# Convolution and gate steps moved into the projection, and delta rule products reordered, in a two-layer hybrid trunk

## The chip, the cores and the metric

One NeuronCore of a Trainium2 chip runs the whole program; nothing is shared with other cores. The metric is device time in microseconds for one execution. The core has five engines that work side by side and meet through semaphores: TensorE (PE, the 128x128 array, with its weight loads shown apart as PEld), VectorE (DVE), ScalarE (ACT), GpSimd (POOL) and SyncE (SP), which here only issues DMAs.

## The reference, cut to what matters

Two layers (`DEPTH = 2`) run over 512 latent and 256 context tokens of width 1024, in fp32. Each layer modulates and projects the tokens to 3088 columns, runs three mixers on slices of them (softmax attention, a gated delta rule, HGRN2), projects back, and then runs a mixture of 16 experts. The second layer gives no output for the context tokens.

```python
q, k, v = split(silu(conv5(cols['dn_qkv'])))          # depthwise, 5 taps, 768 channels
f = lb + (1 - lb) * sigmoid(cols['hg_f'])             # HGRN2 forget gates
# gated delta rule, per head and chunk of 64 tokens (4 heads, 12 chunks, 2 directions)
m    = where(strict, (k*beta) @ k.T * decay, 0)
u, w = solve(I + m, [v*beta, k*beta*exp(cum)])        # unit triangular, 64x64
v_new = u - w @ state
out   = (q*exp(cum)) @ state + (q @ k.T * decay) @ v_new
state = state*exp(c_last) + (k*exp(c_last - cum)).T @ v_new
```

Attention has 8 query heads of 64 over 2 key/value heads. A latent query tile of 128 tokens sees all 768 keys, a context query tile sees the 256 context keys.

## The kernel before, in words

The 768 tokens are six tiles of 128 (tiles 0 and 1 are context, 2 to 5 latent); a tile holds two chunks of 64 tokens, one on partitions 0 to 63 and one on 64 to 127. The program is written by hand, engine by engine: every engine has its own list of functions that runs the stages of a layer in order (modulation, norm, projection, attention, delta rule, HGRN2, output projection, norm, experts), and the order inside a list is the order in which that engine works. Nothing is planned by a tool. What an engine waits for is written as semaphore waits.

**Projection.** `pe_proj` runs 48 units of 8 matmuls (L687) in 8 column groups, through six PSUM banks; `act_proj` (L615) evacuates each unit. Group boundaries fall at units 12 (queries, keys and values done), 24 (the six convolution input tiles `convin` done), 30, 38, 42 (HGRN2 gates `hgc` done) and 48. `dve_attention` prepares queries and keys from unit 12 on, and then waits for unit 48 (`projev` 48) before it does anything else, because its output tile `convout` lay over the second buffer of the weight ring, which the projection still uses.

**Attention.** A unit is one head of one query tile: 48 units in layer 0 (16 of context tiles, then 32 of latent tiles) and 32 in layer 1 (latent only). PE does the scores (L918), six or two transposes of the probabilities (L931) and the product with the values (L941); DVE takes the row maximum (L816) and part of the copy (L825), ACT the exponential (L882) and the rest of the copy (L895). Between them DVE runs one of the 30 convolution steps (L846, L849) in each of the first 30 units and one of the 4 gate steps (L860) in each of the first 4.

**Delta rule.** `act_deltanet` begins with six silu activations over `convout` (L1148) and goes on with the gates (L1149 to L1154). PE waits for the last silu and for the last attention output, then transposes `convout` into token tiles (L1216). DVE squares and sums them (L985, L986). Then for each of the two directions `d`:

- cumulative gates and decays (L1240, L1241), and the gram products (L1251), each followed by DVE work per tile;
- six levels of a doubling scheme for the triangular inverse. In a level, DVE masks the six tiles (L1039), PE multiplies by `small_products` (L1261), ACT copies the result (L1190), PE multiplies twice more (also L1261; once in the last level, not at all in level 0), and DVE subtracts (L1058). The next level's masks come after all six subtractions, in DVE's own order;
- the solution `Y` with 128 columns (L1261 again), copied by ACT (L1194);
- the transition matrices (L1312, L1314, L1317), taken up by DVE (L1068) and ACT (L1202, L1204), then 11 dependent steps over the chunks (L1327, L1079);
- the outputs: per tile the products with the state (L1351, L1353), DVE's fresh values (L1092 to L1098), and the product with the local attention matrix (`apply_values`, L1261 again), added by DVE (L1107, L1109).

All of these products are 64x64 blocks: contraction over 64 partitions (the lower or upper half of the rows of the array) and an output on 64 partitions (the lower or upper half of its columns). The trace shows two matmul instructions, each with its own weight load, for one fp32 product. So a call of `small_products` with 8 products is 16 instructions, and a level of 18 calls is 288. `HB[0]` and `HB[1]` are the two halves. In `small_products` both the row half and the column half are `HB[par]`: before the change four products in a row go to one half, then four to the other.

**What follows.** HGRN2 (L1532 and on), the output projection (L1602) and the experts (L1775, L1803) are not touched.

## Time and profile before

| | us |
|---|---|
| median of 3 runs | 4424.52 |
| range of these runs | 4422.88 to 4425.82 |
| the profiled execution, its own time | 4431.7 |
| span from first to last instruction in it | 4429.9 |

| engine | busy us | share | instructions |
|---|---|---|---|
| PE | 3673.1 | 83% | 24115 |
| PEld | 2632.4 | 59% | 24115 |
| DVE | 2318.7 | 52% | 3029 |
| ACT | 1813.0 | 41% | 2325 |
| POOL | 340.9 | 8% | 100 |

Busy time is the union of an engine's instructions. PE's ends are modelled, so an instruction that has started 0.1 us after another overlaps it, and a busy PE is not PE at its peak; how many instructions are done in a stretch says more. PEclk is the clock that TensorE is granted, as a share of 2.4 GHz; it has two levels, 1.0 and 0.5, and a value between them is a mean over a stretch. An idle time in brackets is that of the engine just before the row, with what ended it.

### The profile page before, as it was taken

The numbers are of one execution on the slowest core, as the hardware profiler recorded it, in microseconds if no ns is written. First come the engines' busy times: TensorE is split into PE (matmuls) and PEld (weight loads), VectorE is DVE, ScalarE is ACT, GpSimd is POOL, SyncE is SP. The second block draws the span as 40 slices with busy tenths as digits, with TensorE's granted clock in tenths as the row PEclk, the third lists the DMA queues.
The fourth block names the chain that finished last, engine by engine and source line by source line (L and its number), as shares of the span: only waits on it lengthen the run. The fifth ranks groups of instructions, "written<-read, shape, count | busy, mean of one in ns | idle before, by whom it ended". The sixth has DMA issues, their size and how long they took to land.

```text
span 4429.9 us, 59181 instructions
## 1 busy us (share of the span) xinstructions
PE 3673.1 (83%) x24115; PEld 2632.4 (59%) x24115; DVE 2318.7 (52%) x3029; ACT 1813.0 (41%) x2325; POOL 340.9 (8%) x100
## 2 busy tenths in 40 slices
PE   6999997776849889988888999887767577887777
PEld 1565777775526666666634657687664366666666
DVE  0112325558446777777731203345583577777767
ACT  1112222113126677777621112311232467767766
POOL 0000000000011111111100000000000112121111
PEclk9998557685879999999999995576757788888888
DMA  7210000000147888888863100000002688878775
GB/s 256 75 39 19 0 1 2 2 2 2 39 167 289 307 327 318 307 306 309 303 220 120 53 19 1 1 2 2 2 2 85 239 292 316 317 294 301 297 299 210
DMA packets 180696, 680.12 MB, mean 154 GB/s; under 512 B 15435, under 2 KB 25759, under 8 KB 180383
## 3 DMA queue, kind: packets, MB, share of 16 engines
q1 hardware_dynamic: 166088, 637.81, 37.8%
q0 software_dynamic: 6144, 20.98, 2.0%
q10 hardware_dynamic: 8283, 18.67, 1.1%
q8 instruction: 144, 2.36, 0.2%
q14 instruction: 37, 0.30, 0.0%
HBM read 656.44 MB, written 20.97 MB: 153 GB/s over the span
## 4 chain that ended last, share of the span: by engine, by line
PE 61%; DVE 16%; DMA 9%; issue 7%; ACT 6%; ACTq 1%; SPq 0%; DVEq 0%; POOL 0%; PEldq 0%
PE ps L687 11%; PE ps L1803 11%; PE ps L1775 8%; DMA gu<-in_moe_w_up 7%; PE ps L1261 6%; PE ps L918 4%; PE ps L941 4%; PE ps L1602 3%; DVE down_lo L2010 3%; ACT hi L1865 3%; DVE gu_lo L2010 2%; PE ps L641 2%; DMA arena<-in_w_mod 2%; PE ps L931 2%; PE ps L1810 1%
## 5 line engine op out<-in xcount | busy, mean ns | idle before, releaser
L2010 DVE TENSOR_TENSOR gu_lo<-gu,hi 128x2816 fp32r<-128x2816 f32 x256 | 782.7, 3087 | 354.3 <-ACT hi L1865 354.3
L1865 ACT ACTIVATE hi<-gu 128x2816 fp32r<-128x2816 f32 x256 | 640.4, 2549 | 136.0 <-DMA gu<-in_moe_w_up 127.3
L1775 PE MATMUL ps<-hi,xsplit 128*96 128x512 f32 (+3 forms) x2304 | 576.4, 397 | 99.7 <-ACT hi L1865 88.2
L1775 PEld LDWEIGHTS ps<-hi,xsplit 128*96 128x96 f32 (+1 forms) x2304 | 411.8, 183 | 230.6 <-ACT hi L1865 108.2
L2010 DVE TENSOR_TENSOR down_lo<-down,hi 128x1024 fp32r<-128x1024 f32 (+1 forms) x256 | 417.5, 1654 | 172.5 <-ACT hi L1865 172.5
L687 PE MATMUL ps<-arena 128*128 128x512 f32 (+2 forms) x1536 | 501.7, 488 | 7.1 <-PE ps L687 4.3
L1775 PE MATMUL ps<-gu_lo,xsplit 128*96 128x512 f32 (+3 forms) x1536 | 416.4, 410 | 85.9 <-DVE gu_lo L2010 85.2
L687 PEld LDWEIGHTS ps<-arena 128*128 128x128 f32 x1536 | 290.5, 190 | 217.1 <-issue 191.7
L1775 PEld LDWEIGHTS ps<-gu_lo,xsplit 128*96 128x96 f32 (+1 forms) x1536 | 282.0, 192 | 194.6 <-DVE gu_lo L2010 133.2
L1865 ACT ACTIVATE hi<-down 128x1024 fp32r<-128x1024 f32 (+1 forms) x256 | 343.6, 1373 | 123.4 <-PE ps L1803 123.2
L1261 PE MATMUL ps<-arena 64*64 64x64 f32 (+1 forms) x6080 | 266.1, 234 | 27.0 <-DVE arena L1039 21.5
L1261 PEld LDWEIGHTS ps<-arena 64*64 64x64 f32 x6080 | 258.5, 140 | 31.8 <-DVE arena L1039 24.3
L2095 POOL DMA_INDIRECT arena<-xn_rows,row_of x32 | 78.4, 2451 | 2514.2 <-DVE row_of L2001 2505.3
L816 DVE TENSOR_REDUCE nmax<-ps 128x1 f32<-128x768 f32 (+1 forms) x80 | 68.0, 850 | 349.5 <-PE ps L918 349.5
L615 ACT ACTIVATE arena<-ps 128x256 f32<-128x256 f32 (+3 forms) x132 | 49.7, 403 | 445.6 <-PE ps L687 445.5
L941 PEld LDWEIGHTS ps<-arena 128*128 128x128 f32 x832 | 183.3, 329 | 54.1 <-issue 48.8
L641 PE MATMUL ps<-arena,condT 128*2 128x512 f32 x384 | 173.6, 606 | 44.6 <-DMA arena<-in_w_mod 21.7
L918 PE MATMUL ps<-arena 64*128 64x256 f32 (+1 forms) x288 | 202.3, 850 | 2.8 <-ACT arena L874 2.8
L1532 PE MATMUL ps<-arena 64*64 64x64 f32 x2688 | 130.7, 315 | 85.5 <-DVE arena L1413 85.5
L941 PE MATMUL ps<-arena 128*128 128x64 f32 x832 | 198.4, 426 | 3.3 <-ACT arena L895 3.3
L1532 PEld LDWEIGHTS ps<-arena 64*64 64x64 f32 x2688 | 122.5, 219 | 93.5 <-issue 55.8
L882 ACT ACTIVATE arena<-ps,nmax 128x768 f32<-128x768 f32 (+1 forms) x80 | 65.3, 816 | 227.7 <-DVE nmax L816 227.6
(292 smaller groups left out, 4986.6 us busy)
## 6 DMA issues: line engine op xcount, KB each, us to landing
gu<-in_moe_w_gate SPq DMA_DIRECT2D x256, 704.0 KB, 6.1
gu<-in_moe_w_up SPq DMA_DIRECT2D x256, 704.0 KB, 8.0
down<-in_moe_w_down SPq DMA_DIRECT2D x64, 2048.0 KB, 7.9
arena<-in_w_mod SPq DMA_DIRECT2D x24, 2048.0 KB, 7.7
down<-in_moe_w_down SPq DMA_DIRECT2D x32, 1536.0 KB, 9.8
arena<-in_w_in SPq DMA_DIRECT2D x6, 2048.0 KB, 7.6
arena<-in_w_out SPq DMA_DIRECT2D x4, 2048.0 KB, 9.8
arena<-in_w_in SPq DMA_DIRECT2D x4, 1536.0 KB, 7.3
```

The costliest lines, as they stand in the source:

```text
L641: ins = nc.tensor.matmul(ps[0:2, g % 2, :], lhsT=cT[:, f, :], rhs=w[:, f, :], start=(f == 0), stop=(f == KT - 1))
L687: ins = nc.tensor.matmul(out, lhsT=lhs, rhs=rhs, start=(f == 0), stop=(f == KT - 1))
L918: ins = nc.tensor.matmul(ps[:, b + n0 // 512, 0:n], lhsT=qkT[part, j, qt * P:(qt + 1) * P], rhs=qkT[part, 4, n0:n0 + n], start=True, stop= ...
L931: ins = nc.tensor.transpose(out, prob[u % 2][:, kt * P:(kt + 1) * P], ident)
L941: ins = nc.tensor.matmul(ps[:, 6 + u % 2, 0:HD], lhsT=probT[u % 2][:, kt * P:(kt + 1) * P], rhs=vtok[:, kt, kv * HD:(kv + 1) * HD], start= ...
L1261: ins = nc.tensor.matmul(ps[HB[par], bank, c0 + width * h:c0 + width * (h + 1)], lhsT=lhs[HB[par], i, h, :], rhs=rhs(par, h), start=True, ...
L1532: ins = nc.tensor.matmul(ps[HB[c % 2], 2 * (n % 3) + hb, c // 2 * HD:c // 2 * HD + HD], lhsT=a, rhs=b, start=True, stop=True)
L1602: ins = nc.tensor.matmul(ps[:, u % 6, :], lhsT=yT[:, f, i * P:(i + 1) * P], rhs=w[:, f, :], start=(f == 0), stop=(f == KT - 1))
L1775: ins = nc.tensor.matmul(ps[0:lhs.shape[1], 3 * m + b, 0:n], lhsT=lhs, rhs=w[:, c0 + 512 * b:c0 + 512 * b + n], start=(row == 0 and stage ...
L1803: ins = nc.tensor.matmul(ps[0:lhs.shape[1], 3 + half, :], lhsT=lhs, rhs=w[:, c0:c0 + 512], start=(ft == 0 and stage == 0 and n == 0), stop ...
L1865: nc.scalar.activation(hi_part(u), whole(u), ACT.Copy).then_inc(hi_a.sem, 1)
L2010: nc.vector.tensor_tensor(lo_part(u), whole(u), hi_part(u).bitcast(F32), ALU.subtract) \
```

## The change

The convolution steps and the gate steps of DVE leave the attention loop. All 30 convolution steps now follow the preparation of queries and keys, after a wait for unit 24, and the 4 gate steps follow a wait for unit 42. The six silus move from the head of `act_deltanet` into `act_proj`, ahead of unit 42. For that `convout` gets a place of its own instead of lying over the weight ring, and `rope2` and `sq_dn` move with it. Layer 0 takes the latent query tiles (2 to 5) first and the context tiles (0, 1) last; layer 1 keeps its order. The loops of four groups of products are turned, so that consecutive products go to different halves of the array. The products themselves, their operands and their number stay as they are.

```diff
-        rope2 = view(extra, 640)
+        rope2 = view(36752, 640)
...
-        convout = view(10752, 6, 772)
+        convout = view(38984, 6, 772)
         dt = view(0, NT, 768)
-        sq_dn = view(extra, NT, 512)
+        sq_dn = view(7680, NT, 512)
...
+                if u == 42:                                                   # act_proj
+                    for j in range(6):
+                        act.wait_ge(conv.sem, conv.n(layer, 24 + j + 1))
+                        nc.scalar.activation(convout[:, j, :], convout[:, j, :], ACT.Silu).then_inc(convact.sem, 1)
...
-            qt, h = divmod(u + 48 - attn_units(layer), NQ)                    # attn_unit
+            qt, h = divmod(u + NQ * NT_CTX, NQ)
+            qt %= NT
...
-            dve.wait_ge(projev.sem, projev.n(layer, 48))                      # dve_attention
+            dve.wait_ge(projev.sem, projev.n(layer, 24))
...
+            for n in range(30):
+                conv_step(n)
+            dve.wait_ge(projev.sem, projev.n(layer, 42))
+            for u in range(4):
+                f = hgc[:, 2 + u, :]
+                nc.vector.tensor_scalar(f, f, omlT[:, layer, u:u + 1], lbT[:, layer, u:u + 1], ALU.mult, ALU.add) \
+                    .then_inc(f_v.sem, 1)
...
             for u in range(attn_units(layer)):
-                if u < 30:
-                    conv_step(u)
-                if u < 4:
-                    f = hgc[:, 2 + u, :]
-                    nc.vector.tensor_scalar(f, f, ...).then_inc(f_v.sem, 1)
...
-            for j in range(6):                                                # act_deltanet
-                act.wait_ge(conv.sem, conv.n(layer, 24 + j + 1))
-                nc.scalar.activation(convout[:, j, :], convout[:, j, :], ACT.Silu).then_inc(convact.sem, 1)
...
                     for hb in range(2):                                       # gram products, L1251
-                        for par in range(2):
-                            c = 2 * i + par
-                            for pair in range(2):
+                        for pair in range(2):
+                            for par in range(2):
+                                c = 2 * i + par
...
                 def small_products(bank, c0, lhs, rhs, i, width=64):
-                    for par in range(2):
-                        for h in range(DNH):
+                    for h in range(DNH):
+                        for par in range(2):
                             ins = nc.tensor.matmul(ps[HB[par], bank, c0 + width * h:c0 + width * (h + 1)],
                                                    lhsT=lhs[HB[par], i, h, :], rhs=rhs(par, h), start=True, stop=True)
...
                         for pair in range(2):                                 # transitions, L1312 to L1317
                             for hb in range(2):
-                                h = 2 * pair + hb
-                                out = ps[HB[hb], 2 * (i % 2) + par, :]
+                                h, out = 2 * pair + hb, ps[HB[hb], 2 * (i % 2) + par, :]
                                 nc.tensor.matmul(out[:, 64 * pair:64 * pair + 64], lhsT=vke[HB[par], i, h, HD:2 * HD],
                                                  rhs=TR[HB[par], i, 1, h, :], start=True, stop=True)
+                            for hb in range(2):
+                                h, out = 2 * pair + hb, ps[HB[hb], 2 * (i % 2) + par, :]
...
+                            for hb in range(2):
+                                h, out = 2 * pair + hb, ps[HB[hb], 2 * (i % 2) + par, :]
...
                     for hb in range(2):                                       # outputs, L1351 and L1353
-                        for par in range(2):
-                            c = 2 * i + par
-                            for pair in range(2):
-                                out = ps[HB[par], 2 * (i % 2) + hb, :]
+                        for pair in range(2):
+                            for par in range(2):
+                                out, c = ps[HB[par], 2 * (i % 2) + hb, :], 2 * i + par
                                 nc.tensor.matmul(out[:, 64 * pair:64 * pair + 64], lhsT=ykT[HB[hb], i, pair, par, :],
                                                  rhs=S[HB[hb], c, pair, :], start=True, stop=True)
+                            for par in range(2):
+                                out, c = ps[HB[par], 2 * (i % 2) + hb, :], 2 * i + par
```

## Rows read from the trace of the kernel before

**Rows 1.** The page: busy time by engine; granted clock in 40 slices.
```profile
PE 3673.1 (83%) x24115; PEld 2632.4 (59%) x24115; DVE 2318.7 (52%) x3029; ACT 1813.0 (41%) x2325; POOL 340.9 (8%) x100
PEclk9998557685879999999999995576757788888888
```

**Rows 2.** The page: lines of the chain that ended last.
```profile
PE ps L687 11%; PE ps L1803 11%; PE ps L1775 8%; DMA gu<-in_moe_w_up 7%; PE ps L1261 6%; PE ps L918 4%; PE ps L941 4%; PE ps L1602 3%; DVE down_lo L2010 3%; ACT hi L1865 3%; DVE gu_lo L2010 2%; PE ps L641 2%; DMA arena<-in_w_mod 2%; PE ps L931 2%; PE ps L1810 1%
```

**Rows 3.** Windows (us, PE, PEld, DVE, ACT, POOL busy, clock, DMA): attention, delta rules.
```profile
396.00:665.00 269.00, 264.29 (x862) 184.68 (x862) 99.02 (x226) 72.40 (x160) 0.00 (x0) 0.52 0.00 1
665.00:991.00 326.00, 256.08 (x4772) 240.38 (x4772) 173.01 (x493) 65.27 (x175) 0.00 (x0) 0.77 0.01 2
2862.00:3190.00 328.00, 258.57 (x4580) 242.91 (x4580) 165.69 (x466) 65.11 (x175) 0.00 (x0) 0.72 0.01 2
```

**Rows 4.** Groups by line (busy us, mean ns | idle before): a convolution step.
```profile
L849 DVE SCALAR_TENSOR_TENSOR arena<-arena,rowsT 128x772 f32<-128x772 f32 x48 | 48.7, 1014 | 0.0
```

**Rows 5.** Windows in attention: units with a convolution step, units without.
```profile
450.00:460.00 10.00, 10.00 (x29) 6.29 (x29) 4.64 (x10) 2.07 (x4) 0.00 (x0) 0.50 0.01 2
560.00:570.00 10.00, 10.00 (x29) 6.29 (x28) 2.70 (x8) 2.19 (x4) 0.00 (x0) 0.50 0.01 2
```

**Rows 6.** Timeline (start, us, row, idle before), ACT: the first copy of unit 42.
```profile
361.19 0.38 ACT L615 ACTIVATE arena<-ps 128x256 f32<-128x256 f32 x1 [6.81 <-PE ps L687]
```

**Rows 7.** Timeline, layer 0: from the last attention output into the delta rule.
```profile
663.18 4.53 ACT L1148 ACTIVATE arena<-arena 128x772 f32<-128x772 f32 x6
664.85 0.28 DVE L832 TENSOR_SCALAR arena<-ps,rinv 128x64 f32<-128x64 f32 x1 [2.70 <-PE ps L941]
667.85 3.55 PE L1216 MATMUL ps<-const,arena 128*128 128x128 f32 x18 [3.11 <-ACT arena L1148]
670.80 0.24 ACT L1154 ACTIVATE gb<-gb 128x48 f32<-128x48 f32 x1
672.09 0.69 DVE L985 TENSOR_TENSOR arena<-arena 128x512 f32<-128x512 f32 x1
```

**Rows 8.** Windows of direction 0, layer 0: levels and solution, transitions, outputs.
```profile
719.35:791.19 71.84, 65.14 (x1536) 63.86 (x1536) 35.07 (x77) 15.11 (x36) 0.00 (x0) 0.96 0.01 3
791.19:811.27 20.08, 14.41 (x289) 13.76 (x289) 13.60 (x49) 4.71 (x24) 0.00 (x0) 0.65 0.01 2
823.29:839.73 16.44, 14.52 (x288) 14.27 (x289) 10.50 (x38) 0.00 (x0) 0.00 (x0) 0.76 0.01 2
```

**Rows 9.** Timeline, PE: level 0, a middle level, the last, the solution; layer 1.
```profile
719.35 6.70 PE L1261 MATMUL ps<-const,arena 64*64 64x64 f32 x96 [4.31 <-DVE arena L1039]
739.15 11.02 PE L1261 MATMUL ps<-arena 64*64 64x64 f32 x288 [1.11 <-DVE arena L1039]
775.56 7.86 PE L1261 MATMUL ps<-arena 64*64 64x64 f32 x192 [1.11 <-DVE arena L1039]
784.02 6.48 PE L1261 MATMUL ps<-arena 64*64 64x128 f32 x96 [0.60 <-DVE arena L1058]
2948.85 12.42 PE L1261 MATMUL ps<-arena 64*64 64x64 f32 x288 [1.11 <-DVE arena L1039]
```

**Rows 10.** Narrow windows of PE, 0.33 us after first start: L1261, then L1327.
```profile
719.67:719.78 0.10, 0.10 (x4) 0.50 0.00 0
811.60:811.70 0.10, 0.10 (x8) 0.50 0.00 0
```

**Rows 11.** Timeline, PE, bursts in other orders: L1327, L1532, L1552.
```profile
811.27 0.69 PE L1327 MATMUL ps<-arena 64*64 64x64 f32 x8 [3.31 <-ACT arena L1204]
1036.07 8.02 PE L1532 MATMUL ps<-arena 64*64 64x64 f32 x192 [0.34 <-DVE arena L1413]
1048.78 1.19 PE L1552 MATMUL ps<-arena 64*64 64x64 f32 x32 [0.21 <-ACT arena L1510]
```

**Rows 12.** Groups by line: DVE's subtraction in a level.
```profile
L1058 DVE TENSOR_TENSOR arena<-arena,ps 128x512 f32<-128x512 f32 x96 | 66.1, 688 | 102.8 <-PE ps L1261 102.8
```

**Rows 13.** Timeline, DVE: fresh values of the third tile wait for PE.
```profile
830.88 0.29 DVE L1092 TENSOR_TENSOR arena<-arena,ps 128x128 f32<-128x128 f32 x1 [1.36 <-PE ps L1353]
```

More of the change, by code:

```diff
@@ L810, in dve_attention, with conv_step @@
             nc.vector.memset(ss[:, 60:61], 0.0).then_inc(qk_ready.sem, 1)
+            nc.vector.memset(convin[:, :, 0:2], 0.0)
+            nc.vector.memset(convin[:, :, 258:262], 0.0)
+            link(nc.vector.memset(convin[:, :, 774:776], 0.0))
+            dve.wait_ge(projev.sem, projev.n(layer, 24))
+            def conv_step(n):
+                k, j = divmod(n, 6)
+                w = rowsT[:, layer * 30 + n:layer * 30 + n + 1]
+                if k == 0:
+                    ins = nc.vector.tensor_scalar(convout[:, j, :], convin[:, j, 0:772], w, None, ALU.mult)
+                else:
+                    dve.wait_ge(conv.sem, conv.n(layer, n - 5))
+                    ins = nc.vector.scalar_tensor_tensor(convout[:, j, :], convin[:, j, k:k + 772], w,
+                                                         convout[:, j, :], ALU.mult, ALU.add)
+                ins.then_inc(conv.sem, 1)
+            for n in range(30):
[5 more added lines that the diff above has]
+                    .then_inc(f_v.sem, 1)
             def row_max(u):
@@ L833, in finish @@
                                         None, ALU.mult).then_inc(attn_y.sem, 1)
-            nc.vector.memset(convin[:, :, 0:2], 0.0)
-            nc.vector.memset(convin[:, :, 258:262], 0.0)
-            link(nc.vector.memset(convin[:, :, 774:776], 0.0))
-            dve.wait_ge(projev.sem, projev.n(layer, 48))
-            def conv_step(n):
-                k, j = divmod(n, 6)
-                w = rowsT[:, layer * 30 + n:layer * 30 + n + 1]
-                if k == 0:
-                    ins = nc.vector.tensor_scalar(convout[:, j, :], convin[:, j, 0:772], w, None, ALU.mult)
-                else:
-                    dve.wait_ge(conv.sem, conv.n(layer, n - 5))
-                    ins = nc.vector.scalar_tensor_tensor(convout[:, j, :], convin[:, j, k:k + 772], w,
-                                                         convout[:, j, :], ALU.mult, ALU.add)
-                ins.then_inc(conv.sem, 1)
             row_max(0)
             for u in range(attn_units(layer)):
-                if u < 30:
-                    conv_step(u)
-                if u < 4:
-                    f = hgc[:, 2 + u, :]
-                    nc.vector.tensor_scalar(f, f, omlT[:, layer, u:u + 1], lbT[:, layer, u:u + 1], ALU.mult, ALU.add) \
-                        .then_inc(f_v.sem, 1)
                 if u + 1 < attn_units(layer):
```

## The prediction

> **What bounds the kernel now.** I read the page first. PE is busy for 83% of the span, and no other engine passes 52%; of the granted clock the reader is to see the 5s in slices 5, 6, 10, 25, 26 and 30: there TensorE has 1.2 GHz and not 2.4 [rows 1]. The chain of waits is mostly PE's; the lines that the change touches hold L1261 at 6% and L918, L941, L931 at 10% together [rows 2]. So I asked for windows by stage. Attention: PE busy 264.3 of 269.0 us at a mean clock of 0.52. Delta rule: 256.1 of 326.0 us at 0.77 in layer 0, 258.6 of 328.0 at 0.72 in layer 1 [rows 3]. No DMA runs in either. Whatever PE or the chain saves there moves all that follows by the same amount, since the experts' loads start only after the output projection. Then the timelines, for which wait ends last at each seam.
>
> **Part 1: convolution and gate steps leave attention.** A step costs DVE 1.014 us or less [rows 4], 30 of them at most 30 us per layer. In attention they are covered: a stretch with steps has PE busy 10.00 of 10 us and 29 matmuls, one without has the same 10.00 and 29, while DVE falls from 4.64 to 2.70 [rows 5]. Their removal there is worth nothing in the steady state. I allow 0.3 us in each layer for the first units, in which DVE's row maximum queues behind them; that is inside the rounding below. In the projection DVE sits idle after the preparation of the queries, PE needs only ACT's evacuations, and 24 units of PE work lie between unit 24 and attention, one of which alone holds ACT idle for 6.81 us [rows 6]. 30 us of steps and four gate steps end well before that. Cost 0; if that cover were gone, up to 30 us a layer. No DMA is moved, and no queue of SP or POOL is passed.
>
> **Part 2: the silus.** Six take 4.53 us, and 1.28 us more for a table load [rows 7]. Ahead of unit 42 ACT is idle for 6.81 us, waiting for PE [rows 6]; 5.8 us fit, and the table load for silu that unit 42 pays now serves both. Were they late, PE has six banks and stops only when an evacuation is five units behind. Cost 0. At the delta rule's head they are on the path: the last attention output ends at 664.85 + 0.28 = 665.13, and the transposes of L1216 start at 667.85 [rows 7], 2.7 us later. ACT then loads a table for Exp (1.28), which it would still hold from attention, and one for Ln. Next late after the change is the chain over the gates: three short DVE operations after 665.13 (some 0.25 us each), an exponential like L1154 (0.24), one load (1.28) and L1154 itself. By this estimate L1154 ends at about 667.7 and not 671.04, and L985 starts at 668.7 for 672.09. Gain 3.4 us a layer, **6.8 us**. From there DVE bounds the stretch, and nothing else is given back.
>
> **Part 3: latent tiles first, layer 0 only.** The units and their products are the same, and PE is full between first and last. What can change is PE's idle time at the two ends, 269.0 - 264.3 = 4.7 us in all [rows 3], so the effect lies between -4.7 and +4.7. A long unit first exposes a longer maximum and exponential, a short one last leaves less to drain. I take **-1.5 us**.
>
> - *Middle levels*, 4 per direction, 16 in all: 288 x 0.029 + 0.3 (the last one's own run) = 8.7 us for 11.02. The 1.11 us ahead of each (DVE's last subtraction 0.69, then the first mask 0.42) stays. DVE's subtractions, 6 x 0.69 [rows 12], and ACT's copies fit in the shorter level. 16 x 2.35 = **37.6**.
> - *Last level*: 192 x 0.029 + 0.3 = 5.9 for 7.86; 4 x 1.9 = **7.6**.
> - *Level 0*: 96 in 6.70, mostly at half clock, 70 ns; alternating 96 x 0.054 + 0.4 = 5.6 us, with DVE's two operations a tile nearly as late. 4 x 1.1 = **4.4**.
> - *Solution*, 128 columns: 96 in 6.48, 67.5 ns; 96 x 0.056 + 0.3 = 5.7, and ACT, busy for 15.1 of 71.8 us here [rows 8], keeps up. 4 x 0.9 = **3.6**.
> - *Transitions*: PE 14.4 and DVE 13.6 of 20.1 us [rows 8]: the two take turns over two pairs of banks. A shorter PE turn (about 0.4 us) counts on every second tile: **4 x 1 = 4**.
> - *Outputs*: 16.4 us, PE 14.5, DVE 10.5 [rows 8]; the third tile's fresh values wait 1.36 us for PE [rows 13]. PE's turn of 48 instructions at up to 70 ns is 2.4 to 3.4 us; at L1532's 42 ns it is 2.0, and DVE's 10.5/6 = 1.75. I take 2.2 us less in each direction, minus 0.7 for a clock that may not rise here as it does now (mean 0.76): 4 x 1.5 = **6**.
> - *Gram products*: DVE is late on both sides of each tile. 0, between -1 and +1.
>
> Sum of part 4: 63.2 us. In transitions and outputs only the column halves alternate, the rows stay. L1552 does just this and runs 32 instructions in 1.19 us [rows 11], so I count them as above. A rule of the Trainium skill speaks against it: "TensorE: Matmul & The Clock Gate", Part 3, has it that a weight load overlaps running matmuls only when its group of rows differs. By the rule these two items would give nothing and the sum would be 10 us smaller. The rule disagrees with L1552 as this trace has it.
>
> **The clock.** The same middle level took 12.42 us in layer 1, against 11.02, where the clock fell to half for a while, after the 1.11 us pause between levels [rows 9]. The change keeps these pauses and brings them closer together (every 9.8 us, not 12.1), so I expect a few more such falls: 3 at 1.4 us, **+4 us**.
>
> **The sum.** -6.8 - 1.5 - 63.2 + 4 = -67.5 us. The profiled execution took 4431.7 us (span 4429.9), so it would take 4364. It is 7.2 us above the median of the runs; the same difference on the median 4424.5 gives **4357 us**. Bounds of the main term: at 27 ns instead of 29 some 10 us more, at 34 ns some 25 us less.
>
> **Rivals.**
>
> - *Instructions can't be fed that fast.* A level would be bound by PE's issue and not by the halves. For it: nothing in the trace sustains 29 ns over 288 pairs; against it: L1532 keeps the array fuller over 192. At 36 ns part 4 falls to some 15 us, with 6.8 and 1.5: 4401 us. Chance 0.10.
> - *The order is already undone by overlap, or only the row halves matter.* Without the two items of fixed rows: 4367, inside the first forecast's range, chance 0.10. With no gain from order at all, 8.3 us remain: 4416, which is -0.19%. Chance 0.03.
> - *Slower: the clock leaves the levels.* The clock is low in attention though PE is busy there for 98%. In the levels it is at 0.96 over 71.84 us [rows 8]. If the denser, shorter levels with the same pauses no longer held it, a middle level would take 288 x 0.054 + 0.3 + 1.11 = 17 us for 12.1, the last +2.7, the solution +4: 26 us a direction, 104 in all, less 20 for the rest: 4509 us. It decides from the point where some 45% of the levels' time runs at half clock. Against it: levels with a 1.11 us pause keep the full clock now in layer 0. Chance 0.04.
>
> **How the numbers follow.** The forecast has 0.73: 4357, own range 4342 to 4378. With the rivals, 4340 to 4400 leaves out about 2 in 10. A difference of 0.2% (9 us) is about what a measurement can tell from none. Faster: all of the forecast, the first rival and the fixed rows, 0.92. Same: 0.03. Slower: 0.05.
>
> **What would show it.** A middle level of 8.4 to 9.0 us with 288 matmuls of L1261 after a pause of still 1.11; L985 about 3.6 us after the last attention output instead of 7.0; DVE busy in the projection and at 2.7 of 10 us in attention; the first attention unit long in both layers; full clock through the levels. It is wrong if a level stays above 10 us, if PE waits for a projection evacuation near unit 42, or if the levels' mean clock falls below 0.8.

## The result, and the profile after

The changed kernel took 4225.42 us (median of four runs: 4223.52, 4225.41, 4225.44, 4380.44), the kernel before on the same chip 4423.7. The ratio is 0.9552, 95% interval 0.9533 to 0.957: 198 us less, where 67.5 were forecast. The direction was right and the time fell outside the range. Each kernel shows two or three separate values, some 90 to 130 us apart, because in each run each of the two attentions has TensorE either at 2.4 GHz or, from its first microseconds on, at 1.2 GHz; the ratio compares the changed kernel's runs with the higher clock in layer 0 with runs of the kernel before that had it in neither layer. The profiled executions show this directly; for a run without a profile, which attention kept the clock is concluded from its time. The experiments are about that.

The page of the profiled execution (4225.41 us, span 4223.6): the engines' busy times, and TensorE's clock in 40 slices.

```profile
PE 3462.4 (82%) x24115; PEld 2456.5 (58%) x24115; DVE 2321.5 (55%) x3029; ACT 1806.0 (43%) x2321; POOL 350.4 (8%) x100
PEclk9999986858799999999899975587557787888888
```

PE has as many instructions as before and is busy 211 us less [rows 1]. Of the two 5s that stood in slices 5 and 6 none is left; those of layer 1's attention (slices 25 and 26) stay. The chain of waits gives less to the small products, now L1266, and to attention, now L949, L926 and L939, than it did [rows 2]; here it is by engine and by line:

```profile
PE 58%; DVE 18%; DMA 9%; issue 7%; ACT 6%; ACTq 1%; SPq 0%; DVEq 0%; POOL 0%; PEldq 0%
PE ps L692 12%; PE ps L1812 11%; PE ps L1784 8%; DMA gu<-in_moe_w_up 7%; PE ps L1266 5%; PE ps L949 3%; PE ps L1611 3%; PE ps L926 3%; DVE down_lo L2019 3%; DVE gu_lo L2019 3%; ACT hi L1874 3%; PE ps L646 3%; DMA arena<-in_w_mod 2%; PE ps L939 2%; PE ps L1819 1%
```

Its lines of attention come to 8% (they were 10%) and L1266 to 5% (6%). Windows by stage show more (us; busy time of PE, PEld, DVE, ACT, POOL; the mean clock; DMA): attention and delta rule of layer 0, then of layer 1.

```profile
399.06:545.66 146.60, 142.91 (x862) 102.99 (x862) 71.70 (x193) 68.08 (x157) 0.00 (x0) 1.00 0.00 1
545.66:850.50 304.84, 217.56 (x4772) 199.16 (x4773) 183.53 (x507) 65.38 (x173) 0.00 (x0) 0.74 0.01 2
2475.61:2701.00 225.39, 221.78 (x735) 158.22 (x735) 55.52 (x129) 56.20 (x109) 0.00 (x0) 0.52 0.00 1
2701.00:2997.60 296.60, 212.45 (x4582) 195.13 (x4583) 176.45 (x481) 65.64 (x173) 0.00 (x0) 0.74 0.01 2
```

Layer 0's attention falls from 271.5 us (396.3 to 667.8) to 146.6, with the clock at 1.00 for all of it and not 0.52 [rows 3]. That is 125 us. The silus account for 2.7 of them and the order of units for about 1; the other 121 come with the clock, and no term of the forecast holds them. Layer 1's attention has the same stream and gained 3 us (228.2 before), the silus again. The delta rule lost 31 us in layer 0 and 42 in layer 1; the forecast had some 33 a layer for the whole of it, of which 2.7 of the silus' 3.4 fall in the attention window. So the part that was worked out came about as said, and one stage did something else.

The delta rule's parts. A timeline of PE through levels and solution of layer 0's first direction (start, us, instruction, count, idle time before):

```profile
596.62 1.97 PE L1266 MATMUL ps<-const,arena 64*64 64x64 f32 x32 [4.31 <-DVE arena L1047]
599.05 3.44 PE L1266 MATMUL ps<-const,arena 64*64 64x64 f32 x64 [0.46 <-DVE arena L1055]
603.42 8.85 PE L1266 MATMUL ps<-arena 64*64 64x64 f32 x288 [0.93 <-DVE arena L1047]
613.39 8.85 PE L1266 MATMUL ps<-arena 64*64 64x64 f32 x288 [1.12 <-DVE arena L1047]
...
643.30 6.28 PE L1266 MATMUL ps<-arena 64*64 64x64 f32 x192 [1.12 <-DVE arena L1047]
650.20 5.46 PE L1266 MATMUL ps<-arena 64*64 64x128 f32 x96 [0.62 <-DVE arena L1066]
```

A middle level takes 8.85 us for 11.02, 30.7 ns an instruction, and the pause ahead of it is still 1.12 us [rows 9]. The windows of the same direction: levels with solution, transitions, outputs.

```profile
596.62:656.34 59.72, 52.42 (x1536) 50.40 (x1536) 34.99 (x77) 15.09 (x36) 0.00 (x0) 0.95 0.02 4
656.34:675.05 18.71, 11.26 (x288) 10.50 (x289) 13.59 (x49) 4.71 (x24) 0.00 (x0) 0.69 0.01 2
687.07:700.75 13.68, 10.82 (x288) 10.11 (x289) 10.28 (x38) 0.00 (x0) 0.00 (x0) 0.74 0.01 2
```

They stood at 71.84, 20.08 and 16.44 [rows 8]. The seam from attention to delta rule, last output (L863) to first square (L993):

```profile
545.32 0.28 DVE L863 TENSOR_SCALAR arena<-ps,rinv 128x64 f32<-128x64 f32 x1 [0.38 <-PE ps L949]
545.66 2.19 PE L1221 MATMUL ps<-const,arena 128*128 128x128 f32 x18 [0.45 <-DVE arena L863]
546.61 1.28 ACT L1159 ACT_TABLE_LOAD   x1
549.19 0.69 DVE L993 TENSOR_TENSOR arena<-arena 128x512 f32<-128x512 f32 x1
```

From the end of L863 to L993 it is 3.6 us; it was 7.0 [rows 7]. One table load is left of the two that stood there. In the projection the steps and silus run while PE works, in groups by line from 145 to 399 us (busy, mean ns, idle before):

```profile
L830 DVE SCALAR_TENSOR_TENSOR arena<-arena,rowsT 128x772 f32<-128x772 f32 x24 | 22.5, 1017 | 0.0
L601 ACT ACTIVATE arena<-arena 128x772 f32<-128x772 f32 x6 | 4.5, 833 | 0.0
```

The projection lasts 253.8 us with them and without: free, as forecast.

Now the head of attention in the changed kernel, twice in one execution: layer 0 (three windows) and layer 1 (three windows), each the pause before the first scores, the first scores, and what follows.

```profile
402.56:403.97 1.41, 0.00 (x1) 0.00 (x1) 0.00 (x0) 1.39 (x5) 0.00 (x0) 1.00 0.00 0
403.97:407.60 3.63, 2.84 (x9) 1.42 (x9) 1.71 (x2) 2.24 (x3) 0.00 (x0) 1.00 0.00 0
407.60:411.27 3.67, 3.67 (x22) 2.69 (x23) 1.59 (x3) 1.76 (x4) 0.00 (x0) 1.00 0.02 4
2479.08:2480.48 1.40, 0.00 (x0) 0.00 (x0) 0.00 (x0) 1.38 (x5) 0.00 (x0) 1.00 0.00 0
2480.48:2482.79 2.31, 2.31 (x7) 1.28 (x8) 0.71 (x1) 1.25 (x1) 0.00 (x0) 1.00 0.00 0
2482.79:2486.00 3.21, 2.83 (x10) 1.78 (x9) 1.51 (x3) 2.23 (x5) 0.00 (x0) 0.50 0.00 0
```

The streams are the same: PE idle for 1.4 us while ACT copies queries and keys, then the same eight score instructions. In layer 0 the clock stays; in layer 1 it falls to 0.50, 2.31 us after the first scores, and stays there to the end of the stage, 218 us in which PE is busy for 99% of the time. Before the change it fell in layer 0 too, 3.29 us after its first scores.

### The profile page after: what moved, and what is told of

It is laid out like the page before. It is cut to its first block, busy times and chain, and to the rows that moved or that the text cites. A ratio compares the mean times of both kernels' runs of the same rounds, so it can differ in the third digit from the quotient of the medians.

```text
span 4223.6 us, 59177 instructions
## 1 busy us (share of the span) xinstructions
PE 3462.4 (82%) x24115; PEld 2456.5 (58%) x24115; DVE 2321.5 (55%) x3029; ACT 1806.0 (43%) x2321; POOL 350.4 (8%) x100
## 4 chain that ended last, share of the span: by engine, by line
PE 58%; DVE 18%; DMA 9%; issue 7%; ACT 6%; ACTq 1%; SPq 0%; DVEq 0%; POOL 0%; PEldq 0%
PE ps L692 12%; PE ps L1812 11%; PE ps L1784 8%; DMA gu<-in_moe_w_up 7%; PE ps L1266 5%; PE ps L949 3%; PE ps L1611 3%; PE ps L926 3%; DVE down_lo L2019 3%; DVE gu_lo L2019 3%; ACT hi L1874 3%; PE ps L646 3%; DMA arena<-in_w_mod 2%; PE ps L939 2%; PE ps L1819 1%
## 5 line engine op out<-in xcount | busy, mean ns | idle before, releaser
L692 PEld LDWEIGHTS ps<-arena 128*128 128x128 f32 x1536 | 290.5, 190 | 217.1 <-issue 191.8
L1266 PE MATMUL ps<-arena 64*64 64x64 f32 (+1 forms) x6080 | 207.7, 225 | 31.6 <-DVE arena L1047 21.6
L1266 PEld LDWEIGHTS ps<-arena 64*64 64x64 f32 x6080 | 197.6, 137 | 40.0 <-DVE arena L1047 24.4
L1541 PEld LDWEIGHTS ps<-arena 64*64 64x64 f32 x2688 | 122.5, 219 | 93.5 <-issue 55.8
L949 PEld LDWEIGHTS ps<-arena 128*128 128x128 f32 x832 | 137.8, 255 | 38.5 <-issue 29.4
L926 PE MATMUL ps<-arena 64*128 64x256 f32 (+1 forms) x288 | 151.6, 657 | 2.8 <-ACT arena L882 2.8
L949 PE MATMUL ps<-arena 128*128 128x64 f32 x832 | 150.4, 347 | 2.4 <-ACT arena L903 2.3
L2126 POOL DMA_INDIRECT out<-arena,row_of x16 | 112.2, 7011 | 441.5 <-DVE arena L2033 441.5
```

Source lines behind the costliest of these rows:

```text
L692: ins = nc.tensor.matmul(out, lhsT=lhs, rhs=rhs, start=(f == 0), stop=(f == KT - 1))
L926: ins = nc.tensor.matmul(ps[:, b + n0 // 512, 0:n], lhsT=qkT[part, j, qt * P:(qt + 1) * P], rhs=qkT[part, 4, n0:n0 + n], start=True, stop= ...
L949: ins = nc.tensor.matmul(ps[:, 6 + u % 2, 0:HD], lhsT=probT[u % 2][:, kt * P:(kt + 1) * P], rhs=vtok[:, kt, kv * HD:(kv + 1) * HD], start= ...
L1266: ins = nc.tensor.matmul(ps[HB[par], bank, c0 + width * h:c0 + width * (h + 1)], lhsT=lhs[HB[par], i, h, :], rhs=rhs(par, h), start=True, ...
L1541: ins = nc.tensor.matmul(ps[HB[c % 2], 2 * (n % 3) + hb, c // 2 * HD:c // 2 * HD + HD], lhsT=a, rhs=b, start=True, stop=True)
L2126: nc.gpsimd.indirect_dma_start(out=table, out_offset=bass.IndirectOffsetOnAxis(ap=row_of[0:rows_e, e:e + 1].bitcast(U32), axis=0), in_=ye[ ...
```

## The experiments

Four theories. **U**: the order of units; long units first leave PE fewer pauses. **V**: the empty DVE, whose steps held up the first row maxima. **C**: chance, how the start of attention falls in time. And, from the second set on, **P**: PE's pauses at the head decide, and afterwards attention holds whichever clock it finds. Times differ by a few us between sets, so each kernel is set against the kernel before in its own set. "Both at half" means both attentions at half clock.

### First set: one part of the change at a time

`e1`: before, with the new order of the products.

```diff
-                    for par in range(2):          # small_products; gram, transitions and outputs likewise
-                        for h in range(DNH):
+                    for h in range(DNH):
+                        for par in range(2):
```

> The kernel before with the new order of the products alone (gram, small products, transitions, outputs); convolution steps, silus and unit order as before. All theories of attention say that nothing happens there: layer 0 attention at about 271 us and half clock. The delta rule should lose what it lost in the whole change less the silus: 31.3 + 41.7 us in the stages of layers 0 and 1, of which about 3.4 a layer are the silus, so 66 us: 4424 - 66 = 4358 us. If the change's delta rule gain came instead from freeing it of the silus and of a clock that was already higher when it began, this run stays above 4390.

`e2`: before, with latent tiles first.

```diff
-            qt, h = divmod(u + 48 - attn_units(layer), NQ)
+            qt, h = divmod(u + NQ * NT_CTX, NQ)
+            qt %= NT
```

> The kernel before with latent query tiles first in layer 0, nothing else. Theory U (order of units: long units leave PE fewer pauses in the first microseconds of attention, and the clock, once kept there, stays full for the whole stage): layer 0 attention about 147 us for 271.5, so 4424 - 125 = 4299 us in most runs. Theory V (it is the empty DVE: with convolution and gate steps between the row maxima PE pauses longer at the start): 4423 us, attention stays at half clock. Theory C (chance: how the start of attention falls against the moments at which the clock changes): some runs near 4423 and some near 4299.

`e3`: before, with the steps and silus moved into the projection.

```diff
-            dve.wait_ge(projev.sem, projev.n(layer, 48))
+            dve.wait_ge(projev.sem, projev.n(layer, 24))
...
+            for n in range(30):
+                conv_step(n)
...
```

> The kernel before with convolution steps, gate steps and silus done during the projection; context tiles first as before, old order of the products. Theory U: attention stays at half clock, only the silus' 6.8 us are gained: 4417 us. Theory V: 4424 - 6.8 - 125 = 4292 us. Theory C: a mix of both values.

`e4`: the changed kernel with context tiles first again.

```diff
-            qt, h = divmod(u + NQ * NT_CTX, NQ)
-            qt %= NT
+            qt, h = divmod(u + 48 - attn_units(layer), NQ)
```

> The changed kernel with context tiles first again in layer 0. Theory U: the attention gain goes, 4225 + 125 = 4350 us in all runs. Theory V: 4225 us stays. Theory C: a mix of 4225 and 4350.

Measured, all runs:

| kernel | both at half | one attention kept |
|---|---|---|
| before | 4426.67 to 4443.99 (9 runs) | 4340.12, 4345.4 |
| e1 | 4351.06, 4354.64, 4360.56 | 4253.99 |
| e2 | 4427.16 to 4437.57 (4) | 4305.27, 4309.13 |
| e3 | 4409.87 to 4438.45 (5) | 4338.1 |
| e4 | 4349.42 to 4356.51 (5) | 4247.38 |

V alone falls: e3 with an empty DVE kept layer 0 in none of its six runs. U in its plain form falls too: e2 kept it in two of six. Even the kernel before has runs 90 us below the rest. The profiled run of e3 tells which attention that is:

```profile
397.25:665.90 268.65, 264.67 (x863) 184.79 (x863) 72.70 (x193) 69.51 (x157) 0.00 (x0) 0.51 0.00 1
2645.58:2769.30 123.72, 119.75 (x734) 87.91 (x734) 55.57 (x128) 56.16 (x109) 0.00 (x0) 1.00 0.00 1
```

Layer 1 took 123.7 us. At half clock and with the silus moved, as in e3, this stage takes 225.4 to 225.7 (the changed kernel, e4), so the clock is worth 102 us there. Against their own kernels the kept runs of before and e3 gain less, 88 to 97 us; part of the difference lies in the levels of the delta rule, which took 294.0 us in before's profile and 301.1 in e3's, and the rest isn't resolved. e2's profiled run is the other kind, with layer 0 at 0.99:

```profile
400.87:552.50 151.63, 142.97 (x862) 103.00 (x863) 97.70 (x229) 73.28 (x163) 0.00 (x0) 0.99 0.00 1
```

So something that differs from run to run has a part in it (C), and the order of units shifts the odds. e1's three runs at half have a median of 4354.6, against 4433.5 for the nine of before: the order of the products alone is worth 79 us and not 66.

### Second set: how often, and the pauses

`f1`: the changed kernel again.

> The changed kernel itself once more, for how often each value comes. Theory C+U (whether the clock falls at the start of an attention is a matter of where that start falls in time, and long units first only make keeping it likelier; one layer each): a mix of 4350 us (both attentions at half clock), 4225 (layer 0 kept, -125), about 4247 (layer 1 kept, -104) and perhaps 4120 (both). Theory U alone (long units first always keep layer 0): 4225 in all but stray runs. Like for like, with both attentions at half clock, the change should be worth 4432 - 4352 = 80 us by the kernel with context tiles first.

`f2`: the changed kernel with filler products in both pauses; `f3` with the first alone. They go to a part of PSUM that nobody reads.

```diff
+            def fill(*widths):
+                for n in widths:
+                    nc.tensor.matmul(ps[:, 7, 0:n], lhsT=ident, rhs=qn[:, 0, 0:n], start=True, stop=True)
+            fill(512, 256)                                    # after the transposes of queries and keys
             pe.wait_ge(qktev.sem, qktev.n(layer, 5))
...
+                if u == 0:
+                    fill(256, 128)                            # f2 only
                 turn(u)
```

> The changed kernel with filler products (their output is never read) in TensorE's two pauses at the head of each attention: 512 and 256 columns in the pause of 1.41 us before the first scores, 256 and 128 in that before the first transposes of probabilities. Theory P (those pauses let the clock fall, and a clock once kept stays for the stage): both attentions at full clock in every run, 4350 - 125 - 104 = 4121 us, with no spread over 20 us. Theory N (the fall depends on the chip's moment alone, or on the half-filled score products and not on the pauses): a mix as in the changed kernel, 4225 to 4355.

> The same with filler products only in the first pause. Theory P with the first pause as the one that matters (five of the six falls seen so far came 1.5 to 2.6 us after the first scores, when only this pause lay behind): 4121 us as with both. If the second pause matters too: now and then 4225 or 4250. Theory N: a mix from 4225 to 4355.

`f4`: the first pause made longer.

```diff
+                if p == 4:
+                    for _ in range(2):
+                        link_act(nc.scalar.activation(qkT[:, p, 0:512], ps[:, b, :], ACT.Copy))
                 nc.scalar.activation(qkT[:, p, 0:512], ps[:, b, :], ACT.Copy)
```

> The changed kernel with the first pause made longer by two more copies of 512 columns on ScalarE ahead of the first scores (about 1 us more in each layer). Theory P: the clock falls in both attentions in every run, 4352 + 2 = 4354 us. Theory C+U without a role of the pause: a mix as in the changed kernel.

| kernel | all runs |
|---|---|
| before | 4429.98 to 4448.58 (9), median 4434.99; 4342.62, 4342.77 |
| f1 | 4343.24, 4349.78, 4355.45, 4356.64; 4230.83, 4232.88 |
| f2 | 4124.54 to 4135.88 (6), median 4130.27 |
| f3 | 4115.72 to 4133.22 (6), median 4123.99 |
| f4 | 4350.4 to 4360.54 (4), median 4354.0 |

P holds on both sides. With 1.3 us of filler the clock stayed in both layers in all 12 runs; with 1.25 us more of idle time it fell in both layers in all four. Filling the second pause adds nothing. (Filler both closes a pause and adds products; no run here separates the two.) f3's timeline of PE at the head of layer 1 (L918 is the filler, 0.12 us before the scores), and its two attentions:

```profile
2484.63 3.46 PE L913 MATMUL ps<-const,arena 128*128 128x128 f32 x30 [0.84 <-ACT arena L620]
2487.93 1.46 PE L918 MATMUL ps<-arena,const 128*128 128x512 f32 x4
2489.51 2.84 PE L931 MATMUL ps<-arena 64*128 64x512 f32 x8
...
```

```profile
396.33:542.90 146.57, 144.20 (x867) 103.70 (x867) 71.71 (x193) 68.09 (x157) 0.00 (x0) 1.00 0.00 1
2484.63:2608.40 123.77, 121.04 (x739) 88.57 (x739) 55.57 (x129) 56.15 (x109) 0.00 (x0) 1.00 0.00 1
```

f1 answers how often: the changed kernel kept layer 0 in 2 of 6 runs here and in 3 of 4 in the first measurement. Over all sets layer 0 was kept in 7 of 16 runs with latent tiles first (the changed kernel, f1 and e2) and in none of 49 with context tiles first (before, e1, e3, e4), all without filler. An empty DVE may help: 5 of 10 without steps in attention, 2 of 6 with them, too few to tell. With equal clocks (both at half) the changed kernel takes 4352.6 us for 4435.0, **82 us less**, where the runs of each spread over 13 and 19 us. That is what the change is worth in itself.

### Third set: the change's part in it, the rule on rows, the dips in the levels

The kernel before took 4425.76 to 4436.78 us here (4 runs, median 4429.3) with both attentions at half clock, and 4327.31, 4332.13 and 4335.99 with one kept.

`g1`: the kernel before with f3's filler.

> The kernel before with filler products (512 and 256 columns) in the first pause of each attention and nothing of the change. Theory P (that pause decides, whatever the kernel): layer 1, whose first units are long, is kept at full clock in every run, so 4434 - 100 = 4334 us at most; layer 0 starts with short units, which have two more pauses of 0.79 and 0.56 us before the third unit, so it may still fall. If it is kept too: 4334 - 125 = 4209 us, and the change as such has no part in the attention gain. If layer 0 falls in every run, latent tiles first is what the filler in layer 0 needs.

Measured 4329.07 to 4331.79 (4 runs, median 4330.16). Layer 1 was kept in every run, layer 0 in none: with short units first, the windows are

```profile
397.91:669.40 271.49, 265.63 (x866) 185.30 (x867) 99.76 (x229) 74.99 (x163) 0.00 (x0) 0.51 0.00 1
2641.61:2769.60 127.99, 121.12 (x739) 88.71 (x739) 81.51 (x165) 61.39 (x115) 0.00 (x0) 0.99 0.00 1
```

So latent tiles first has a part after all: with long units at the head the filler held the clock in 40 attentions of 40 (f2, f3, g1's layer 1, g2 and g3), with short ones in none of four. A short unit's scores last 0.56 us for a long one's 1.42. In g1's profile the clock fell 2.79 us after the first scores, with one pause of 0.79 us between them and the fall; a second one, of 0.50, came after it. DVE's convolution steps, which g1 still has in attention, are not the likely cause, since its layer 1 has them too; but context tiles first with filler and an empty DVE was not run.

`g2`: f3 with transitions (L1316 and on) and outputs (L1358, L1362) in their old order.

```diff
-                            for hb in range(2):                     # three loops of two products
-                                h, out = 2 * pair + hb, ps[HB[hb], 2 * (i % 2) + par, :]
+                            for hb in range(2):                     # one loop, three products each
+                                h = 2 * pair + hb
+                                out = ps[HB[hb], 2 * (i % 2) + par, :]
...
```

> The changed kernel with the filler in the first pause, and the loops of the transitions and outputs as before the change: there four columns' halves no longer alternate product by product, while the row half stays fixed in both versions. By the rule that a weight load overlaps only where the row group differs, nothing changes: transitions 18.71 us, outputs 13.5 and 10.3 to 11.0 us, 4124 us. By the column halves as the cause: transitions back to 20.08 us (4 x 1.37), outputs back by one part of their 11.5 us (the other part belongs to the small products), so 4130 to 4141 us.

Measured 4133.64 to 4139.5 (4 runs, median 4137.02), 13 us over f3, which ran in another set; the two delta rules alone take 10 us more in its profile than in f3's. Its windows of transitions and of the outputs of the first direction, then of transitions in layer 1:

```profile
654.39:674.46 20.07, 14.50 (x288) 13.66 (x288) 13.59 (x49) 4.71 (x24) 0.00 (x0) 0.65 0.01 2
686.48:702.46 15.98, 13.93 (x289) 13.69 (x289) 10.45 (x38) 0.00 (x0) 0.00 (x0) 0.75 0.01 2
2714.36:2734.33 19.97, 13.64 (x290) 12.98 (x290) 13.61 (x49) 4.71 (x24) 0.00 (x0) 0.69 0.01 2
```

PE is busy 14.50 us for the same 288 instructions that take it 11.26 in the changed kernel, and 13.64 where the mean clock is the same as there (0.69). The stage lasts 19.97 to 20.09 us in all 20 stretches profiled with the old loops and 18.7 in all 36 with the new ones. Only the order of the column halves differs between the two; the row half stays fixed in both, so a change of the row half isn't needed for the gain.

`g3`: f3 with gram and small products in their old order, and filler between the levels.

```diff
+                    if level >= 2:
+                        for _ in range(2):
+                            nc.tensor.matmul(ps[:, 7, 256:512], lhsT=ident, rhs=cst("lvl0")[:, 0:256], start=True, stop=True)
                     for i in range(NT):
```

> The changed kernel with the first filler, the gram and small products in their old order, and two filler products of 256 columns in each pause of 1.11 us between two levels. In the old order levels and solution took 71.9 us in 3 of 12 stretches and 73.9 to 76.3 in 9, with spells of half clock. Theory L (the old order's sparser stream together with the pauses lets the clock fall): with the pauses filled all four stretches take 71.9 us. If the dips come from the old order's stream alone, several of the four are still at 74 to 76 us.

Two runs, 4167.54 and 4178.05. The four stretches of levels and solution took 71.4, 71.3, 72.0 and 71.2 us, by the same measure as the 71.85 and 59.7 of the two orders. PE's timeline (L1288 is the filler):

```profile
600.27 11.02 PE L1271 MATMUL ps<-arena 64*64 64x64 f32 x288 [0.85 <-DVE arena L1052]
611.22 1.13 PE L1288 MATMUL ps<-const 128*128 128x256 f32 x4
612.41 11.02 PE L1271 MATMUL ps<-arena 64*64 64x64 f32 x288
...
```

With the pauses filled no level dips, and a level still takes its 11.02 us: the filler keeps the clock and leaves the products' own time as it was. The two runs are 49 us over f3's median, and four stretches at 71.5 for 59.6 make 48.

`g4`: f4, where the clock always falls, with a burst of filler ahead of the fifth unit's transposes.

```diff
+                if u == 4:
+                    pe.wait_ge(attn_y.sem, attn_y.n(layer, 3))
+                    fill(448, 448, 448, 448, 448, 448, 448, 448)
                 turn(u)
```

> The changed kernel with the longer pause (which let the clock fall in 4 of 4 runs, 4354 us) and eight filler products of 448 columns ahead of the fifth unit's transposes, in each layer. Theory B (attention's own stream keeps either level: what it finds it holds): the clock rises in the burst and stays; layer 0 about 167 us for 268.6, layer 1 about 144 for 226, 4354 - 183 = 4171 us. Rival (the level is set by the stream itself, and a full clock is lost again after the burst): 4354 + 12 = 4366 us.

Two runs, 4168.06 and 4171.3. Windows of layer 0: up to the fall, the low stretch, the rest; the burst runs from 434.6 to 442.5 us, and the clock rises within it.

```profile
396.58:403.89 7.31, 4.64 (x34) 3.89 (x34) 0.00 (x0) 6.34 (x13) 0.00 (x0) 1.00 0.00 0
403.89:438.03 34.14, 34.14 (x99) 22.64 (x98) 8.51 (x16) 8.30 (x17) 0.00 (x0) 0.50 0.00 0
438.03:565.90 127.87, 126.40 (x749) 89.85 (x747) 63.25 (x177) 54.70 (x130) 0.00 (x0) 1.00 0.00 1
```

99 instructions in 34 us, then 749 in 128, and the same units go on. The level is not set by attention's steady stream, which runs on at either; a burst of products over all 128 rows lifts it for the rest of the stage. That shows the second half of P.

## Why the prediction was wrong, point by point

- **Attention (part 3 and the bound under it).** This is the step that failed. I held that in layer 0 only PE's 4.7 us of idle time could change, "so the effect lies between -4.7 and +4.7", and took the clock of 0.52 as a property of the stage, since PE is busy there for 98% [rows 3]. It is a property of the run: in all 15 attentions profiled that fell, it did so within 3.3 us of the first scores, 14 of them with a pause of 1.4 us or more right ahead of these scores (the other is g1's layer 0); then the level stayed to the end of the stage, but for g4's burst. Measured worth: 121 us in layer 0 (267.4 to 268.6 us at half clock, 146.6 at full, less 1 for the order of units) and 102 in layer 1 (225.4 and 123.8). The page had the hint: the 5s begin where attention does [rows 1], right behind a projection at full clock, and I never asked what PE did just before the fall. Without the clock, latent tiles first is worth about 1.1 us, where I took 1.5: f4's layer 0 took 268.7 us, or 267.4 less its extra 1.25, and with context tiles first it is 268.6 in e3 and 268.4 in e4.
- **Silus (part 2): right.** 2.66 us before the transposes and 0.71 after, 3.37 a layer for 3.4. That is their price behind an attention at half clock. Where attention kept the clock and the silus still followed it, the stretch took 9.1 us (e2, layer 0) and 8.2 (g1, layer 1) in place of 7.0; against the 3.6 after the change the move is worth 5.5 and 4.6 there.
- **Convolution and gate steps (part 1): right.** Nothing in the steady state, nothing in the projection; as a sufficient cause of the clock (theory V) they are ruled out by e3.
- **Order of the products (part 4): mechanism right, sizes near.** At full clock a middle level takes 8.85 us (forecast 8.7), the last 6.28 (5.9), level 0 some 5.9 to 6.1 (5.6), the solution 5.46 (5.7): 71.85 to 59.7 us a direction, 49 us in all for 53.2. Transitions gave 1.37 us each, 5.5 for 4.
- **Outputs: mis-sized.** 11.5 us over the four, for 6. I took 0.7 us off each for a clock that hardly got worse (0.76 and 0.74). By g2 some 8 of the 11.5 belong to the alternating column halves, the rest to the products with the local attention matrix. The gram products gave nothing, as forecast (14.95 us a direction for 14.97).
- **The clock in the levels: wrong sign.** I added 4 us for more frequent falls. In the old order the 16 stretches of four profiled kernels average 74.7 us, with 71.85 the undisturbed value; in the new order 36 stretches lie between 59.3 and 59.9. So the dips cost 11.6 us on average before (6.6 in the profiled execution of the kernel before) and vanish: the denser stream survives the pause of 1.12 us that the sparser one often did not. g3 shows that it takes the pause and the sparse stream together.
- **The rivals.** Issue-bound at 36 ns: out, 30.7 measured. Fixed rows give nothing: out by g2. The rule of the Trainium skill ("TensorE: Matmul & The Clock Gate", Part 3) that a weight load overlaps running matmuls only when the row group differs, taken as a forecast of no gain here, does not agree with these traces; they show the time gained, and not whether it is loads or matmuls that overlap. A clock that leaves the levels: out. That a clock could be gained was among none of them: I had a rival for losing it and no mirror image, though the mean granted clock of the whole execution was 0.806.

The terms as measured at equal clocks: 6.7 + 1.1 + 60.2 + 5.5 + 11.5 = 85 us, against 82 between the medians and 67.5 in the forecast. With both attentions at half clock the changed kernel would stand at about 4341 us beside the 4423.7 of the first measurement, within the range of 4340 to 4400; that attention could run at another clock is what the forecast left out. That f1's four runs (4343 to 4357) lie around 4357 is in part luck: the kernel before took 11 us more in that set. The 82 and the clock's 121 make 203 us, for 198 between the medians. One sum of mine was off by a little: faster is 0.73 + 0.10 + 0.10 = 0.93, and not 0.92. One run of the first four, 4380.44, lies 24 us above the highest of f1's and has no profile; its mean clock was 0.78, where those four had 0.804 to 0.809, so more ran at half clock than the two attentions, and where stays open.

**A version that beats both.** f3, the changed kernel with 1.3 us of filler at the head of each attention: 4124.0 us (4115.7 to 4133.2), beside 4435.0 for the kernel before (0.930) and 4352.6 or 4231.9 for the changed one, and its runs differ by 18 us, not by 121.

**What a start's fate goes with.** In f1's profile and in the one above, one stream held in layer 0 and fell in layer 1, so only the moment differed. The traces show which moment. The clock rises shortly before each projection; windows of the changed kernel ahead of and behind that rise, layer 0 and then layer 1:

```profile
136.00:141.25 5.25, 5.25 (x26) 5.25 (x25) 1.86 (x3) 2.46 (x4) 0.00 (x0) 0.50 0.01 2
141.25:402.56 261.31, 256.90 (x819) 150.62 (x818) 59.02 (x77) 41.12 (x90) 0.00 (x0) 1.00 0.11 37
2211.00:2216.55 5.55, 3.71 (x18) 3.71 (x19) 2.56 (x5) 1.23 (x2) 0.00 (x0) 0.50 0.01 3
2216.55:2482.79 266.24, 260.43 (x837) 153.07 (x836) 60.82 (x80) 44.98 (x96) 0.00 (x0) 1.00 0.11 36
```

All 15 falls came 266.24 us after this rise, whatever the kernel. The first scores don't keep such a distance. Ten profiled attentions have long units first and neither filler nor a longer pause. The four whose first scores came 262.7 to 263.5 us after the rise held, with the point at which others fell lying 2.8 to 3.5 us behind these scores. The six at 263.9 to 264.7 us, with that point 1.5 to 2.3 us behind, fell. With filler five at 263.9 to 264.6 us held, so the filler and not the moment made the difference there. With short units first one at 262.95 us fell (the kernel before, layer 0). This is read from traces; no run shifted a start on purpose.

**Still open.** Why layer 1 held so much more rarely: without filler, latent tiles at the head held in 7 of 16 runs in layer 0 but in 10 of 65 in layer 1. In the profiles its first scores mostly come later after the rise (263.9 us or more in six of seven, layer 0 in none of three), but no run separates the two layers. No kernel had filler in the further pauses of short units.

## What to carry to other kernels

Where the clock is low in a stage whose engine is busy all the time, look at what TensorE did in the last microseconds before the clock fell, and price the other level as a case of its own: an idle microsecond at a seam can cost 100 us behind it, and a microsecond of filler products there can save them. Repeat runs until the separate values show, and compare changes only between runs with the same stages at the same clock, or a change of unit order looks like a gain of 121 us that more than half of the runs (9 of 16) do not have. For small products, let consecutive ones go to different halves of the array, columns alone included.

## What the runs showed of the hardware

- The same stage, with PE busy for 98% of it, took 225 us at half clock and 124 at full clock (layer 1 of the changed kernel, and of f3); behind the moment of the fall neither level changed by itself up to the stage's last products.
- The fall comes 0.3 to 3.3 us after the first scores, never later, in all 15 attentions profiled that fell (four of them in kernels with a longer pause), and each time 266.24 us after the clock's rise ahead of the projection.
- A burst of eight filler products of 448 columns over all 128 rows in the middle of the stage lifted the clock for the rest of it (g4, both layers in its profile).
- With only the column half alternating, 288 instructions kept PE busy for 11.26 us in place of 13.64, at the same mean clock (0.69; the changed kernel and g2).
